# Three of six convolution tiles of the first layer moved from VectorE to TensorE, with shifted copies made by DMA

## The reference

```
def conformer_conv(u, dw, dw_b, ln_g, ln_b):
    a, gate = jnp.split(u, 2, axis=-1)
    v = a * jax.nn.sigmoid(gate)
    v = lax.conv_general_dilated(v, dw[:, None, :], window_strides=(1,),
                                 padding=[(CONV_K - 1, 0)],          # CONV_K = 31
                                 dimension_numbers=('NWC', 'WIO', 'NWC'),
                                 feature_group_count=CONV_W) + dw_b  # depthwise, 768 channels
    return jax.nn.silu(layer_norm(v, ln_g, ln_b))
...
    h = rms_norm(x, norm_mix_g[l])
    u = h @ a_w_in[i]                                                # 1024 -> 1792
    conv_out = conformer_conv(u[..., :2 * CONV_W] + a_b_glu[i], ...)
    qm = rms_norm(u[..., 2 * CONV_W:].reshape(B, S, MEM_HEADS, HEAD_DIM), mem_q_norm_g[l])
    mix = jnp.concatenate([conv_out, memory_attention(qm, mk, mv)], axis=-1)
    x = x + mix @ w_out[l]
    x = x + squared_relu_mlp(rms_norm(x, norm_mlp_g[l]), w_mlp_in[l], w_mlp_out[l])
```

## Time and profile before

| | |
|---|---|
| time of the kernel, median of 3 runs | 1124.65 us (1124.63 to 1126.05) |
| the profiled execution | 1125.16 us, span 1123.3 us |
| PE busy | 1025.1 us (91%) |
| PEld busy | 921.7 us (82%) |
| DVE busy | 816.0 us (73%) |
| ACT busy | 613.1 us (55%) |
| POOL busy | 187.7 us (17%) |
| DMA | 158.28 MB, mean 141 GB/s |

### The profile page before, as it was taken

The page is one execution under the profiler, slowest core; times in us unless marked ns, Lnnn a source line. Parts: engine busy times, 40 slices in busy tenths (PEclk is TensorE's granted clock), DMA queues, the critical chain, the costliest instruction groups (busy, mean ns, idle before and its releaser), DMA issues.

```text
span 1123.3 us, 17425 instructions
## 1 busy us (share of the span) xinstructions
PE 1025.1 (91%) x6610; PEld 921.7 (82%) x6610; DVE 816.0 (73%) x1577; ACT 613.1 (55%) x1148; POOL 187.7 (17%) x87
## 2 busy tenths in 40 slices
PE   4997689999999999779999999999898899999975
PEld 4996568888888888668888888888688899999865
DVE  4799778967668645978797676766546677777775
ACT  5553176745645636655665563565435566546555
POOL 1772001212121000001121212223000000100210
PEclk9997689999999979899999999999978999999988
DMA  8442024655555413014445555522302355554501
GB/s 355 150 165 98 1 74 151 212 200 175 197 174 182 144 62 125 1 38 149 157 178 193 187 188 187 182 90 76 150 1 76 150 188 185 177 193 165 191 30 38
DMA packets 22834, 158.28 MB, mean 141 GB/s; under 512 B 2528, under 2 KB 2784, under 8 KB 4448
## 3 DMA queue, kind: packets, MB, share of 16 engines
q1 hardware_dynamic: 21888, 153.51, 38.1%
q10 hardware_dynamic: 864, 3.66, 0.8%
HBM read 156.12 MB, written 1.05 MB: 140 GB/s over the span
## 4 chain that ended last, share of the span: by engine, by line
PE 69%; DVE 21%; ACT 5%; issue 3%; DMA 1%; DVEq 0%; ACTq 0%; SPq 0%
PE bank L707 66%; DVE obank L2002 5%; DVE split_lo L600 3%; PE obank L707 2%; DVE square_sum L1994 1%; ACT split_hi L592 1%; PE bank L840 1%; ACT probs L1408 1%; ACT L1408 1%; DVE mlp_parts L2002 1%; DVE tmp L2002 1%; DVE probs L1998 1%; DVE hidden_parts L1994 1%; DVE tmp L1994 1%; DMA consts<-in_consts 1%
## 5 line engine op out<-in xcount | busy, mean ns | idle before, releaser
L707 PE MATMUL bank<-act_parts,split_hi 128*128 128x256 f32 (+1 forms) x1632 | 341.0, 305 | 32.5 <-DVE split_lo L600 13.2
L592 ACT ACTIVATE split_hi<-ring 128x1024 fp32r<-128x1024 f32 (+1 forms) x280 | 289.8, 1048 | 126.2 <-PE bank L707 121.3
L600 POOL TENSOR_TENSOR split_lo<-ring,split_hi 128x1024 fp32r<-128x1024 f32 (+1 forms) x75 | 184.2, 2463 | 899.6 <-ACT split_hi L592 899.6
L707 PEld LDWEIGHTS bank<-act_parts,split_hi 128*128 128x128 f32 x1632 | 269.6, 200 | 44.0 <-issue 28.5
L600 DVE TENSOR_TENSOR split_lo<-ring,split_hi 128x1024 fp32r<-128x1024 f32 (+1 forms) x205 | 249.4, 1227 | 41.7 <-ACT split_hi L592 41.1
L707 PE MATMUL bank<-hidden_parts,split_hi 128*128 128x512 f32 (+1 forms) x816 | 266.1, 378 | 2.8 <-DVE split_lo L600 2.1
L707 PE MATMUL bank<-act_parts,split_lo 128*128 128x256 f32 x880 | 255.7, 291 | 0.0
L707 PE MATMUL bank<-hidden_parts,split_lo 128*128 128x256 f32 x752 | 211.5, 281 | 0.0
L707 PE MATMUL bank<-mlp_parts,split_hi 128*128 128x512 f32 x512 | 182.0, 400 | 2.5 <-DVE mlp_parts L2002 2.5
L707 PEld LDWEIGHTS bank<-hidden_parts,split_hi 128*128 128x128 f32 x816 | 148.9, 188 | 34.4 <-DVE split_lo L600 2.7
L707 PEld LDWEIGHTS bank<-act_parts,split_lo 128*128 128x128 f32 x880 | 176.4, 200 | 0.0
(11 more groups left out here) (266 smaller groups left out, 1297.1 us busy)
## 6 DMA issues: line engine op xcount, KB each, us to landing
ring<-in_weights SPq DMA_DIRECT2D x141, 1024.0 KB, 4.9
ring<-in_weights SPq DMA_DIRECT2D x5, 768.0 KB, 4.2
x<-in_x ACTq DMA_DIRECT2D x1, 1024.0 KB, 7.9
y<-in_mem ACTq DMA_DIRECT2D x1, 1024.0 KB, 9.9
out<-x SPq DMA_DIRECT2D x4, 256.0 KB, 2.5
consts<-in_consts ACTq DMA_DIRECT2D x1, 885.0 KB, 12.9
ring<-in_weights SPq DMA_DIRECT2D x1, 512.0 KB, 3.6
consts<-in_consts ACTq DMA_DIRECT2D x1, 260.0 KB, 7.9
```

Source lines behind the costliest of these rows:

```text
L592: nc.scalar.activation(split_hi[:, w % SPLIT, 0:n], src, ACT.Copy).then_inc(sem("high_parts"), 1)
L600: (nc.vector if engine == "vector" else nc.gpsimd).tensor_tensor(split_lo[:, w % SPLIT, 0:n], src, split_hi[:, w % SPLIT, 0:n].bitcast(F32 ...
L707: return nc.tensor.matmul(dst, lhsT, rhs, start=start, stop=stop)
```

## The change

Of the six channel tiles of the convolution, VectorE keeps tiles 0 to 2 (`OWN_CONV = 3`). Tiles 3 to 5 are computed on TensorE. For each of them SyncE's queue issues 16 DMAs (`shifted_copies`), on-chip to on-chip: for each of four shifts s and each quarter j of the 128 channels, 32 rows of `glu`, moved by s tokens, go to partitions 32s to 32s+31 of `shifted`. A product over 128 partitions then covers 32 channels at four neighbouring taps; eight of them cover 31 taps (padded to 32). The stationary operand is a block of four stacked 32 x 32 diagonals (`diagonals`), which GpSimd makes from the taps (`conv_diagonals`). `shifted_taps(n)` issues 8 x 4 products; the four quarters j write four different groups of 32 PSUM partitions of one bank. VectorE adds the bias on the way out (`shifted_sum`).

The rest is order. TensorE does the shifted taps, the memory attention of the first layer and `ln.mean` among the projections of the memory, which before all stood ahead of the attention; the second layer's projection of the values now stands after `ln.mean`; `ln.var` ahead of the transposes of the attention's result. The eight filling products `keep_busy` in front of the convolution part of `out0` go. ScalarE writes the SiLU once (`mix`), and GpSimd makes the rounded copy `act_hi`, which was a second SiLU. The first constant transfer carries 427 columns where it had 520.

TensorE, before, from the last products of the values of layer one on (`split_hi,hidden_parts`): `consts,rc` and `consts,sq` are the head norm's broadcast and sums, and the first `hidden_parts,split_hi` starts the keys of layer two.

The diff, cut to what the prediction speaks of:

```diff
+OWN_CONV = 3
+SHIFTS = 4
+SHIFTED_TAPS = 8
+SHIFTED_COLS = SEQ + SHIFTS * (SHIFTED_TAPS - 1)
...
+            def shifted_copies(n):
+
+                c = OWN_CONV + n
+                sp_.wait_ge(sem("cleared"), 2)
+                sp_.wait_ge(sem("glu.ready"), c + 1)
+                for s in range(SHIFTS):
+                    width = SHIFTED_COLS if s < SHIFTS - 1 else SHIFTED_COLS - SHIFTS
+                    for j in range(4):
+                        sp_.dma_start(shifted[32 * s:32 * s + 32, n, j, 0:width], glu[32 * j:32 * j + 32, c, s:s + width])\
+                           .then_inc(sem(f"conv.shifted{n}"), 16)
+
             for b in range(NBLOCKS):
+                if OWN_CONV + 8 <= b < CONV_TILES + 8:
+                    shifted_copies(b - OWN_CONV - 8)
...
+            def shifted_taps(n):
+
+                pe.wait_ge(sem("conv.diagonals"), 2 + n + 1)
+                pe.wait_ge(sem(f"conv.shifted{n}"), 16 * 4 * SHIFTS)
+                dst = take("conv.sum", n)
+                blocks = diagonals[n].rearrange("p (j k c) -> p j k c", j=4, k=SHIFTED_TAPS)
+                for k in range(SHIFTED_TAPS):
+                    live = slice(0, 32 * min(SHIFTS, TAPS - SHIFTS * k))
+                    for j in range(4):
+                        last = mm(dst[32 * j:32 * j + 32, 0:SEQ], blocks[live, j, k, :],
+                                  shifted[live, n, j, SHIFTS * k:SHIFTS * k + SEQ], k == 0, k == SHIFTED_TAPS - 1)
+                ready(last)
 
...
             head_stat("qm0")
-            linear_tokens("mem_kv0", 2, 2, chunk_of(1))
+            shifted_taps(0)
             head_bcast("qm0")
             head_stat("mk0", 2)
-            linear("mem_kv1", 0, 2, chunk_of(1))
+            shifted_taps(1)
             head_bcast("mk0")
-            linear_tokens("mem_kv1", 2, 2, chunk_of(1))
-            head_stat("mk1", 4)
+            shifted_taps(2)
+            units = UNITS["mem0"]
             wait_emptied(pe, "qm0.bc", 0)
             wait_emptied(pe, "mk0.bc", 0)
+            for n in range(2):
+                scores("mem0", units[n], n)
+            linear_tokens("mem_kv0", 2, 2, chunk_of(1))
+            probs_transposed("mem0", units[0], 0)
+            linear("mem_kv1", 0, 1, chunk_of(1))
+            scores("mem0", units[2], 2)
+            probs_transposed("mem0", units[1], 1)
             wait_emptied(pe, "mem_kv0", 2)
-            attention("mem0")
+            outputs("mem0", units[0], 0)
+            linear("mem_kv1", 1, 1, chunk_of(1))
+            scores("mem0", units[3], 3)
+            outputs("mem0", units[1], 1)
+            head_stat("mk1", 4)
+            dst = take("ln.mean", 0)
+            for c in range(CONV_TILES):
+                if c < OWN_CONV:
+                    pe.wait_ge(sem("conv.done"), c + 1)
+                else:
+                    pe.wait_ge(sem("conv.shifted_done"), c - OWN_CONV + 1)
+                last = mm(dst[:, 0:SEQ], const("ones"), conv[:, c, :], c == 0, c == CONV_TILES - 1)
+            ready(last)
+            for n in (2, 3):
+                probs_transposed("mem0", units[n], n)
+            linear_tokens("mem_kv1", 2, 2, chunk_of(1))
+            for n in (2, 3):
+                outputs("mem0", units[n], n)
+            dst = take("ln.var", 0)
+            for c in range(CONV_TILES):
+                pe.wait_ge(sem("ln.squares"), c + 1)
+                last = mm(dst[:, 0:SEQ], const("ones"), sq[:, c, :], c == 0, c == CONV_TILES - 1)
+            ready(last)
 
...
-            keep_busy(take("out0", SPLIT), 8)
...
-                for dst in (mix, act_hi):
-                    last = do(dst[:, c, :], conv2[:, c, :], ACT.Silu, const("ln_b", c, 1), const("ln_g", c, 1))
-                last.then_inc(sem("mixed0.high"), 1)
+                do(mix[:, c, :], conv2[:, c, :], ACT.Silu, const("ln_b", c, 1), const("ln_g", c, 1)).then_inc(sem("mixed0.value"), 1)
...
+            def conv_diagonals(n):
+
+                tt_(diagonals[n].rearrange("p (b c) -> p b c", c=32), rows(stacked_ident, 32),
+                    bcast(const("dw_shifted", 32 * n, 32), 32), ALU.mult).then_inc(sem("conv.diagonals"), 1)
+
+            wait_inverted(pool, "mix0")
+            conv_diagonals(0)
+            low_parts(2 * SPLIT)
+            conv_diagonals(1)
             low_parts(3 * SPLIT)
+            conv_diagonals(2)
...
+            low_parts(WEIGHTS_OF["out0", SPLIT - 1] + 1)
+            for c in range(CONV_TILES):
+                pool.wait_ge(sem("mixed0.value"), c + 1)
+                nc.gpsimd.tensor_copy(act_hi[:, c, :], mix[:, c, :]).then_inc(sem("mixed0.high"), 1)
...
-                taps(5)
+                taps(4 if c < 4 else 2)
...
+            def shifted_sum(n):
+
+                c = OWN_CONV + n
+                wait_tile(dve, "conv.sum", n)
+                ts(conv[:, c, :], bank("conv.sum", n)[:, 0:SEQ], const("dw_b", c, 1), ALU.add).then_inc(sem("conv.shifted_done"), 1)
+                dve.wait_ge(sem("conv.shifted_done"), n + 1)
+                dve.sem_inc(emptied("conv.sum", n), 1)
+
+            taps(8)
+            invert("qm0", 8)
+            taps(8)
+            normed_heads("qm0", [y[:, t, :] for t in range(2)], [q[:, t, :] for t in range(2)], [const("g_memq0")] * 2)
+            shifted_sum(0)
             invert("mk0", 8)
-            taps(14)
+            taps(8)
             memory_keys(0)
-            taps(12)
-            attention("mem0", finish_plain, lambda w: taps(6))
+            shifted_sum(1)
+            taps(6)
+            shifted_sum(2)
+            unit_maximum("mem0", 0)
+            taps(1)
+            unit_maximum("mem0", 1)
+            taps(9)
+            unit_transposed("mem0", 0)
+            taps(6)
+            unit_maximum("mem0", 2)
+            unit_transposed("mem0", 1)
+            taps(OWN_CONV * (TAPS + 1))
+            unit_maximum("mem0", 3)
+            finish_plain("mem0", ("mem0", "mem", 0, 0))
+            dve.wait_ge(sem("conv.done"), OWN_CONV)
+            dve.wait_ge(sem("conv.shifted_done"), CONV_TILES - OWN_CONV)
+            wait_tile(dve, "ln.mean", 0)
+            for c in range(CONV_TILES):
+                ins = stt(conv2[:, c, :], bank("ln.mean", 0)[:, 0:SEQ], -1.0 / 768, conv[:, c, :], ALU.mult, ALU.add)
+                ins.then_inc(sem("ln.centered"), 1)
+            dve.wait_ge(sem("ln.centered"), CONV_TILES)
+            dve.sem_inc(emptied("ln.mean", 0), 1)
+            for n in (2, 3):
+                unit_transposed("mem0", n)
             invert("mk1", 8)
-            taps(10)
+            finish_plain("mem0", ("mem0", "mem", 1, 0))
+            wait_emptied(dve, "ln.var", 0)
+            settle(nc.vector.reciprocal(tmp2[:, 0, 0:256], tmp[:, 0, 0:256]))
+            for c in range(CONV_TILES):
+                tt_(conv2[:, c, :], conv2[:, c, :], tmp2[:, 0, 0:256], ALU.mult).then_inc(sem("ln.scaled"), 1)
 
```

More of the change, by code:

```diff
@@ L261, in psum_tiles @@
     linear("qm0.stat", 1)
-    linear("mem_kv0", 2, 2)
+    linear("conv.sum", 1)
     linear("qm0.bc", 1)
     linear("mk0.stat", 1)
-    linear("mem_kv1", 2)
+    linear("conv.sum", 1, 1)
     linear("mk0.bc", 1)
+    linear("conv.sum", 1, 2)
+    out.extend(("mem0", "S", n) for n in range(2))
+    linear("mem_kv0", 2, 2)
+    out.append(("mem0", "T", 0))
+    linear("mem_kv1", 1)
+    out.append(("mem0", "S", 2))
+    out.append(("mem0", "T", 1))
+    linear("mem_kv1", 1, 1)
+    out.append(("mem0", "S", 3))
+    linear("mk1.stat", 1)
+    linear("ln.mean", 1)
+    out.extend(("mem0", "T", n) for n in (2, 3))
     linear("mem_kv1", 2, 2)
-    linear("mk1.stat", 1)
-    attention("mem0")
+    linear("ln.var", 1)
     linear("mem0.oT", 2)
     linear("mk1.bc", 1)
-    linear("ln.mean", 1)
-    linear("ln.var", 1)
     linear("out0", 8)
@@ L455, in build @@
             pass
+        with nc.sbuf_tensor("shifted", [128, CONV_TILES - OWN_CONV, 4, SHIFTED_COLS], F32) as shifted:
+            pass
         probs = sb("probs", [128, 3, 512])
@@ L891, in outputs @@
                     last.then_inc(sem("out_ready"), 1)
-            def attention(kind):
-                units = UNITS[kind]
-                scores(kind, units[0], 0)
-                for w in range(len(units) + 2):
-                    if w + 1 < len(units):
-                        scores(kind, units[w + 1], w + 1)
-                    if 1 <= w <= len(units):
-                        probs_transposed(kind, units[w - 1], w - 1)
-                    if w >= 2:
-                        outputs(kind, units[w - 2], w - 2)
+            def shifted_taps(n):
[9 more added lines that the diff above has]
+                ready(last)
             def query_heads_stat(name, first, count):
@@ L1097, in _ @@
                     half_products(dst, w, k, act_parts, k == CONV_TILES, False)
-            dst = take("ln.mean", 0)
-            for c in range(CONV_TILES):
-                pe.wait_ge(sem("conv.done"), c + 1)
```

(49 more changed lines are left out.)

108 lines of the change are left out of this document (46 added, 62 removed).

## The result

The changed kernel takes 1118.42 us (median of 20 runs), the kernel before 1126.01 (20 runs). The ratio is 0.9927, 95% interval 0.9916 to 0.9939: 8.2 us or 0.73% faster, where I had forecast 21.5 and a range that ended at 1113. That ratio leaves out the slow executions, which took 1131 to 1139 us (4 of the 20) and to which the profiled one belongs (1138.12 us, with the granted clock at 0.50 from 378.2 to 443.0 us), so only its first 150 us are read here.

The account below looks back on a forecast made before the run. VectorE's taps bound the stage, then TensorE: 46.1 us of work plus 1.5 for waits ends `ln.var` at 117. With the tail, the first add comes 21.5 us earlier: 1125.16 - 21.5 = 1103.7, so 1103.4 us; 8 in 10: 1097 to 1113.

Parts of the forecast that it names:

- the pace of the copies: SyncE's queue: one issue each 0.43 us, a lot of 16 in 6.9 us, lots ending at 64.9, 72.2 and 79.5.
- my 1.5 above: Allowance in TensorE's sum up to `ln.var` for waits on second keys' squares and the third lot of copies: 1.5 us.
- the wait of at most 3 us for the third lot: Sign in the changed profile: TensorE waits at most 3 us for the third lot, not at all for the first.
- The end of `ln.var`: TensorE's work from 69.3 us, 46.1 us to 115.4, plus 1.5 for waits: `ln.var` ends at 117.
- The tail: From `ln.var` at 117 through root, reciprocal, scalings, rests and output products to the first add at 127.0 or 131.2.
- the half clock behind the gap, of which I took the middle: Fourteen output pairs after TensorE's idle: 9.0 us at half clock, 4.8 at full; gain 19.4 or 23.6, taken as 21.5.
- The products: Shifted taps on TensorE: four strips side by side, 3.5 us a tile, three tiles 10.4 us.
- The 4.3 us: Tile time by the skill's rule on weight-load overlap, making the sum 2.5 us longer; set aside for 3.5.
- Two halves: Nearest trace row, sixteen records of 64-column halves in 1.09 us, taken as showing two strips really parallel.
- VectorE's slack: VectorE ends its taps near 99.5, TensorE comes to `ln.mean` at 101.5: slack 2 us.
- What lies behind the first add: From the first output tile's add to x on, the same instructions run in both kernels, as long as before.
- the copies are late: Rival: late copies or late VectorE replace the taps as the wait; 4 to 8 us more, 1108 to 1112, chance 0.20.

Follow-up runs that it names:

- first lot three times: Changed kernel without the copies for the second and third shifted tile; TensorE multiplies the first tile's copies three times. Ratio 0.9763 to the kernel before.
- two lots: Changed kernel with copies issued one weight load earlier and tiles 4 and 5 sharing 16 copies of two tiles each. Ratio to before 0.9762, again 0.9789.
- strip by strip: Kernel with two lots, with the loop over the four strips outside and that over the eight steps inside. One run, 1121.7 us.
- copies one load earlier: Changed kernel with each lot of copies issued one weight load earlier, ahead of the wait for the ring. Ratio 0.9815 to the kernel before.

## Why the prediction was wrong

The direction and the mechanism were right. The step that failed is the pace of the copies: "a load is issued each 0.43 us (three in 1.29), so a lot of 16 is 6.9 us". It took 10.8, and 11.5 from one lot's start to the next. I took a row of three loads for the pace of 48 copies; the earlier trace rows shows only that a short run of loads goes at 0.43. ScalarE's six loads in a row, the longer row, were in the same trace and would have given 0.50 and lots of 8 us, still too few. And I weighed the resulting wait by itself, "up to 2.7 us late: my 1.5 above", with no price for what a wait does to TensorE's clock. The term of the sum that failed by it is the 1.5 us for waits: the waits measured 11.2. Of the signs that I had named, the wait of at most 3 us for the third lot did not hold (5.44, and 5.76 for the second).

The working of the sum, against the profile:
- **The end of `ln.var`**, forecast 117, was 131.5. The waits were 11.2 us where 1.5 stood: 9.7. Two tiles partly at half clock, 4.93 + 6.04 - 2 x 3.66: 3.65. The first tile began at 70.58 instead of 69.3: 1.3. Together 14.6, which is all of it. The 1.3 lies ahead of everything that the copies touch. From 35 to 46 us TensorE was busy without a break both in the changed kernel and in the one with the first lot three times (first tile at 69.68), but at a mean granted clock of 0.69 against 0.84; at 0.15 of 11 us that is 1.65 us of full clock. The changed kernel's second profile has the 0.69 too (70.75). Neither profile is of an execution near the median, so whether those lose it as well is not shown, nor why the clock was lower.
- **The tail** from there to the add, forecast 10.0 to 14.2 us, was 13.4. The half clock behind the gap, of which I took the middle, was there for the whole of k = 6 and 7 and gone for the six pairs behind. With the copies in time it held for five of the eight pairs, and the tail was 12.3.
- **The products**: 3.5 us a tile forecast, 3.66 measured; and without waits `ln.var` ends at 115.0 in the kernel with two lots, where the sum of durations had 115.4. So the sum of TensorE's work was right to half a microsecond. The 4.3 us, an estimate from the Trainium skill, "TensorE: Matmul & The Clock Gate", part 3 (What overlaps and what doesn't), did not come: this trace does not agree that a weight load hides only where it goes to another group of rows. All these loads go to all 128 rows, and the records of one strip come 0.22 us apart both with loads of 0.11 us (32 columns, in the run strip by strip) and with loads of 0.19 us (128 columns, in the kernel before), which could not be if the load took time of its own. Two halves were a good guide to four quarters.
- **VectorE's slack** of 2 us was 0.5: in the kernel with two lots its last tap and sum end at 100.9, forecast 99.5, and `ln.mean` starts at 101.43, forecast 101.5. That it was enough is partly luck.
- **What lies behind the first add** did not change beyond its spread: 972.7 us from it to the end before, 972.2 and 972.1 in the kernels with copies one load earlier and with the first lot three times, and 966 to 975 in the other profiles of kernels with two lots (990.4 in the profile of the changed kernel, with its 65 us at half clock). So the first add is a good mark to a few us, not to tenths.

The rival "the copies are late" was the case, and its price, 4 to 8 us, was a quarter to a half of the 15 us by which the time missed the forecast. With the copies in time the kernel has the first add at 127.3, in the window of 127.0 to 131.2 that I gave, and runs at 0.976 to 0.979 of the time before, which is 1099 to 1102 us; the forecast of 1103.4 is that kernel's.

## What to carry to other kernels

Price the issue of a train of small DMAs from the longest row of issues in the trace, per DMA, and lay the end of each train beside the time when it is wanted: here 4 us a lot turned into 15 us of the end. Merge copies so that one DMA moves more, and put them ahead of a load that waits for something else. Each stand of TensorE of 4.1 to 6.1 us in the first layer here cost its length and then a half-clock stretch behind it, so price such a stand with both (5.44 us of standing went with 2.4 us more for the next tile), or give TensorE something to do.

## What the runs showed of the hardware

- Issuing copies back to back on the sync queue: 0.59 to 0.60 us busy and 0.63 to 0.64 from one to the next, alike for 32 partitions with 35.5 KB, 32 partitions with 71 KB and 128 partitions with 35.5 KB, with one or two issues of 1.1 to 1.8 us in most lots of 16. A weight load of 1 MB takes 0.33 alone and 0.53 right behind a lot.
- 32-column float32 products of 256 columns, four strips in turn: 64 records in 3.66 us; one strip at a time: 11.50. A factor of 3.1 by the order of two loops. The records of one strip are 0.22 us apart in both.
- TensorE after standing 4.14, 4.96, 5.12, 5.44, 5.76 and 6.12 us in the first layer came back at half clock each time; after 1.80 it stayed at full clock, and so it did where the 4.1 us were filled. The kernel before came back at full clock after 3.04 us (145.10) and was at half from 147.3 on.
- The length of the stand is not all. Further on in the kernel with two lots the clock was 0.50 behind a stand of 1.43 us (482.4) and 1.00 behind one of 2.01 (743.0). And with the copies one load earlier it fell with no stand at all: 0.5 us into `ln.mean` (4.52 us for 2.84 from 108.26 on), behind 2.9 us of small products (scores, 64-column outputs, 2-column sums); in the other kernels the same products left the clock alone. Why there and not elsewhere stays open.
